# Gate and up blocks of the second feed-forward as Strassen units of seven half-size products

## Time and profile before

| | us |
|---|---|
| median of 3 runs | 1340.04 |
| lowest, highest | 1339.39, 1341.31 |
| span of the profiled execution | 1339.4 |
| its own time | not stated on the page; the median is 0.6 above the span |
| TensorE busy | 1322.1 (99%) |
| VectorE, ScalarE, GpSimd busy | 639.0, 418.3, 279.9 |

### The profile page before, as it was taken

One profiled execution on the slowest core, in us unless ns is written; L12 is line 12 of the kernel. 1 busy time (PEld: TensorE's weight loads), 2 busy tenths in 40 slices (PEclk: granted clock), 3 DMA queues, 4 the chain that ended last, 5 costly groups with the idle time before them and its releaser, 6 DMA issues.

```text
span 1339.4 us, 24243 instructions
## 1 busy us (share of the span) xinstructions
PE 1322.1 (99%) x10659; PEld 1285.2 (96%) x10659; DVE 639.0 (48%) x790; ACT 418.3 (31%) x577; POOL 279.9 (21%) x388
## 2 busy tenths in 40 slices
PE   7999999999999999999999999999999999999997
PEld 6999999999999999999999986899999999999997
DVE  4445246543644636468574546344433334433343
ACT  6222122221223422474434133333221122212233
POOL 0000789988702201000013000130000000000011
PEclk9999999999999999999999999999999999999998
DMA  6533332222223342126334747122322232222221
GB/s 185 111 83 96 86 88 79 80 82 84 88 64 95 84 83 61 48 80 163 103 93 130 242 179 247 37 80 81 91 81 79 80 90 84 79 79 83 79 60 71
DMA packets 227144, 130.24 MB, mean 97 GB/s; under 512 B 22240, under 2 KB 221392, under 8 KB 227024
## 3 DMA queue, kind: packets, MB, share of 16 engines
q1 hardware_dynamic: 223168, 123.66, 32.2%
q10 hardware_dynamic: 3872, 5.04, 1.1%
HBM read 121.72 MB, written 5.78 MB: 95 GB/s over the span
## 4 chain that ended last, share of the span: by engine, by line
PE 95%; DVE 2%; ACT 1%; issue 1%; DMA 0%; SPq 0%; DVEq 0%; ACTq 0%
PE PS L642 92%; PE PS L1183 1%; DMA AR<-in_x_prompt 0%; PE PS L719 0%; ACT wh L1315 0%; ACT gua L1375 0%; DVE Hs L1903 0%; PE PS L1161 0%; PE PS L801 0%; PE PS L1134 0%; DVE AR L2203 0%; PE PS L1269 0%; PE PS L812 0%; PE PS L866 0%; DVE Hs L1828 0%
## 5 line engine op out<-in xcount | busy, mean ns | idle before, releaser
L1315 ACT ACTIVATE wh<-raw 128x1024 fp32r<-128x1024 f32 (+1 forms) x192 | 200.3, 1043 | 742.0 <-PE PS L642 742.0
L642 PE MATMUL PS<-xh,wh 128*128 128x288 f32 x1792 | 390.9, 300 | 0.1
L642 PE MATMUL PS<-xh,wl 128*128 128x288 f32 x1792 | 384.2, 296 | 0.0
L642 PE MATMUL PS<-xl,wh 128*128 128x288 f32 x1792 | 384.0, 296 | 0.0
L642 PEld LDWEIGHTS PS<-xh,wh 128*128 128x128 f32 x1792 | 288.4, 189 | 2.6 <-issue 1.1
L642 PEld LDWEIGHTS PS<-xh,wl 128*128 128x128 f32 x1792 | 289.2, 189 | 0.0
L642 PEld LDWEIGHTS PS<-xl,wh 128*128 128x128 f32 x1792 | 289.0, 189 | 0.0
L1681 DVE TENSOR_TENSOR wl<-raw,wh 128x1024 fp32r<-128x1024 f32 (+1 forms) x192 | 245.9, 1280 | 73.9 <-ACT wh L1315 72.8
L642 PE MATMUL PS<-yh,wh 128*128 128x288 f32 x960 | 206.5, 297 | 0.0
L642 PE MATMUL PS<-yh,wl 128*128 128x288 f32 x960 | 205.6, 296 | 0.0
L642 PE MATMUL PS<-yl,wh 128*128 128x288 f32 x960 | 205.4, 296 | 0.0
(11 more groups left out here) (315 smaller groups left out, 988.0 us busy)
## 6 DMA issues: line engine op xcount, KB each, us to landing
raw<-in_w_ffn_gu SPq DMA_DIRECT2D x88, 512.0 KB, 3.8
raw<-in_w_ffn_down SPq DMA_DIRECT2D x32, 512.0 KB, 4.0
raw<-in_w_in SPq DMA_DIRECT2D x16, 512.0 KB, 4.0
raw<-in_w_ckv SPq DMA_DIRECT2D x16, 512.0 KB, 3.8
raw<-in_w_ffn_down SPq DMA_DIRECT2D x16, 384.0 KB, 3.4
Hs<-in_cache_mem_k SPq DMA_DIRECT2D x6, 1024.0 KB, 6.2
raw<-in_w_out SPq DMA_DIRECT2D x8, 512.0 KB, 4.1
raw<-in_w_cq SPq DMA_DIRECT2D x8, 512.0 KB, 4.5
```

Of the source, the lines that this page charges most:

```text
L642: return e.matmul(out, lhsT, rhs, start=start, stop=stop, **kw)
L1315: e.activation(wh[:, n % 2, 0:K * P], raw[:, n % 4, 0:K * P], ACT.Copy).then_inc(w_hi, 1)
```

## The change

Each pair of a gate and an up block of FFN2 becomes a **unit**. Its matrix is seen as two by two: low and high half of k (four tiles each) against gate and up; the tokens as low and high half of k against low and high half of the tokens (288). Seven products of half k and half the tokens (`product`, 4 x 3 matmuls of 288 columns) replace eight.

- Weight combinations: GpSimd forms four sums of 128 x 512 per unit (`weight_sums`), two units ahead; ScalarE rounds seven operands of 512 into a ring of ten (`weight_high`) and VectorE subtracts (`weight_low`), one unit ahead.
- Token combinations: four per k tile (`tok_h`, `tok_l`), formed once by VectorE during `w_co` (`norm3`), split by `tokens_high` and `tokens_low`.
- Results: products accumulate in banks 0 to 3; ScalarE copies intermediate states of bank 0 three times and of bank 1 once (`keep`: e1, e5, e2, e3), VectorE adds (`unit`). `gs` is multiplied by R as before, `us` is not: GpSimd multiplies `act` by R instead (`gate_by_root`).
- `xh` and `xl` of the low half of k hold only the low half of the tokens; `rms(3)` moves behind the fourth product of unit 0, and on ScalarE behind all splits of unit 1.
- `load` waits for the unit's splits and sums. Block counters skip the units (`seq`). 23 semaphores that were used once are merged into three counters, one per engine (`POINT`), counted in the order of their engine; the waits stand where they stood.

In the diff the indentation is cut by eight columns.

```diff
+RING, HK = 10, KD // 2
+ring_h = [view(ARr, 16 * T + 1024 * i, HK, P) for i in range(RING)]
+ring_l = [view(ARr, 16 * T + 1024 * i + 512, HK, P) for i in range(RING)]
+ring_hf = [t.bitcast(F32) for t in ring_h]
+xg = view(MM, 7168, HK, T)
+tok_h, tok_l = view(ARr, 0, HK, 4, TH), view(ARr, 8 * T, HK, 4, TH)
+tok_hf, tok_f = tok_h.bitcast(F32), view(AR, 8 * T, HK, 4, TH)
+spare = [view(Xs, i * KD * T, KD, T)[:, 0:HK, TH:T] for i in range(2)]
+sum1, sum2, sum3, sum4 = (spare[i // 2][:, :, i % 2 * P:i % 2 * P + P] for i in range(4))
+e1, e2, e3, e5 = (sq[:, i // 2, i % 2 * TH:i % 2 * TH + TH] for i in range(4))
...
-        add("gu", A[f"w_ffn{which}_gu"], 2 * nf, KD, 0, (f0 * P, F + f0 * P, P), f0=f0 + (which - 1) * FT)
+        add("gu", A[f"w_ffn{which}_gu"], 2 * nf, KD, 0, (f0 * P, F + f0 * P, P), f0=f0 + (which - 1) * FT, seven=which == 2)
...
+def seq(n):
+    return sum(1 for g, i in blocks[0:n] if not g.get("seven"))
+units = [n for n, (g, i) in enumerate(blocks) if g.get("seven") and i % 2 == 0]
+FIRST_UNIT = [0]
+for nf in FGROUPS:
+    FIRST_UNIT.append(FIRST_UNIT[-1] + nf)
...
-        if n >= 4:
-            e.wait_ge(w_lo, n - 1)
+        if n >= 4 and (n - 4) // 2 * 2 in units:
+            v = units.index((n - 4) // 2 * 2)
+            e.wait_ge(S("lo_ok"), 7 * v + (7 if n % 2 else 3))
+            e.wait_ge(S("sum_ok"), 4 * v + 4)
+        elif n >= 4:
+            e.wait_ge(w_lo, seq(n - 4) + 3)
...
+    def weight_sums(v, gate_times_r=None):
+        g, u = units[v], units[v] + 1
+        g_lo, g_hi = (raw[:, g % 4, a:a + 512].rearrange("p (k n) -> p k n", k=HK) for a in (0, 512))
+        u_lo, u_hi = (raw[:, u % 4, a:a + 512].rearrange("p (k n) -> p k n", k=HK) for a in (0, 512))
+        e.wait_ge(raw_in[g % 4], 16 * (g // 4 + 1))
+        e.wait_ge(raw_in[u % 4], 16 * (u // 4 + 1))
+        if v:
+            e.wait_ge(S("lo_ok"), 7 * v - 5)
+        TTT(sum1, u_lo, u_hi, ALU.add).then_inc(S("sum_ok"), 1)
+        e.wait_ge(S("sum_ok"), 4 * v + 1)
+        if v:
+            e.wait_ge(S("lo_ok"), 7 * v - 3)
+        TTT(sum2, sum1, g_lo, ALU.subtract).then_inc(S("sum_ok"), 1)
+        e.wait_ge(S("sum_ok"), 4 * v + 2)
+        if v:
+            e.wait_ge(S("lo_ok"), 7 * v - 2)
+        TTT(sum4, g_hi, sum2, ALU.subtract).then_inc(S("sum_ok"), 1)
+        if gate_times_r is not None:
+            gate_by_root(gate_times_r)
+        if v:
+            e.wait_ge(S("lo_ok"), 7 * v - 1)
+        TTT(sum3, g_lo, u_lo, ALU.subtract).then_inc(S("sum_ok"), 1)
+    def gate_by_root(v):
+        e.wait_ge(g_act, FT + v + 1)
+        TTT(act[:], act[:], R[:], ALU.mult).then_inc(S("act_r"), 1)
+    sums(3, between=lambda: weight_sums(0))
+    for i in range(3):
+        if i:
+            weight_sums(FIRST_UNIT[i])
+        weight_sums(FIRST_UNIT[i] + 1)
+        for v in range(FIRST_UNIT[i], FIRST_UNIT[i + 1]):
+            if v + 2 < FIRST_UNIT[i + 1]:
+                weight_sums(v + 2, gate_times_r=v)
+            else:
+                gate_by_root(v)
     sums(4)
...
+    def product(m, b, x_h, x_l, begins, ready=None):
+        e.wait_ge(S("lo_ok"), m + 1)
+        for k in range(HK):
+            if ready:
+                e.wait_ge(ready[0], ready[1] + k + 1)
+            for wi, (w, x) in enumerate(((ring_h, x_h), (ring_h, x_l), (ring_l, x_h))):
+                last = mm(bank(b, TH), w[m % RING][:, k, :], x[:, k, :], start=begins and k == 0 and wi == 0,
+                          stop=k == HK - 1 and wi == 2, skip_group_check=True)
+        last.then_inc(S("pr_done"), 1)
+    def unit(v):
+        n, first = units[v], v in FIRST_UNIT
+        lo, hi, lo_t, hi_t = slice(0, HK), slice(HK, KD), slice(0, TH), slice(TH, T)
+        if first:
+            e.wait_ge(ps_free, seq(n) + 1)
+        e.wait_ge(S("e_ok"), 4 * v)
+        product(7 * v, 0, xh[:, lo, lo_t], xl[:, lo, lo_t], True, ready=(x_lo, 24) if v == 0 else None)
+        if v:
+            e.wait_ge(S("c_ok"), 4 * v - 2)
+        product(7 * v + 1, 1, tok_h[:, :, 0, :], tok_l[:, :, 0, :], True, ready=(S("t1_lo"), 0) if v == 0 else None)
+        if first:
+            e.wait_ge(ps_free, seq(n) + 2)
+        if v:
+            e.wait_ge(S("c_ok"), 4 * v - 3)
+        product(7 * v + 2, 3, xh[:, hi, lo_t], xl[:, hi, lo_t], True, ready=(x_lo, 28) if v == 0 else None)
+        e.wait_ge(S("e_ok"), 4 * v + 1)
+        product(7 * v + 3, 0, tok_h[:, :, 2, :], tok_l[:, :, 2, :], False, ready=(S("t_lo"), 0) if v == 0 else None)
+        if v == 0:
+            rms(3)
+        e.wait_ge(S("e_ok"), 4 * v + 2)
+        product(7 * v + 4, 1, xh[:, hi, hi_t], xl[:, hi, hi_t], False)
+        e.wait_ge(S("e_ok"), 4 * v + 3)
+        product(7 * v + 5, 0, tok_h[:, :, 1, :], tok_l[:, :, 1, :], False)
+        if v:
+            e.wait_ge(S("c_ok"), 4 * v)
+        product(7 * v + 6, 2, tok_h[:, :, 3, :], tok_l[:, :, 3, :], True)
+    for i, nf in enumerate(FGROUPS):
+        for v in range(FIRST_UNIT[i], FIRST_UNIT[i + 1]):
+            unit(v)
+        g, v = groups[FFN2 + 2 * i + 1], FIRST_UNIT[i + 1]
+        for b in range(KD):
+            if b == 0:
+                e.wait_ge(S("e_ok"), 4 * v)
+                e.wait_ge(S("c_ok"), 4 * v - 2)
+            elif b == 1:
+                e.wait_ge(S("c_ok"), 4 * v)
+            dense(g["n0"] + b, b % 2, nf, yh, yl, ready=(hid_lo, FT + FIRST_UNIT[i]) if b == 0 else None,
+                  each=turn_last if i == 2 and b == KD - 1 else None)
...
+    def weight_high(v, j):
+        g, u, m = units[v], units[v] + 1, 7 * v + j
+        src = (raw[:, g % 4, 0:512], sum1, raw[:, g % 4, 512:1024], sum2, sum4, sum3, raw[:, u % 4, 512:1024])[j]
+        if j in (0, 2):
+            e.wait_ge(raw_in[g % 4], 16 * (g // 4 + 1))
+        elif j == 6:
+            e.wait_ge(raw_in[u % 4], 16 * (u // 4 + 1))
+        else:
+            e.wait_ge(S("sum_ok"), 4 * v + (0, 1, 0, 2, 3, 4)[j])
+        if m >= RING:
+            e.wait_ge(S("pr_done"), m - RING + 1)
+        if j in (0, 2, 6):
+            src = src.rearrange("p (k n) -> p k n", k=HK)
+        e.activation(ring_h[m % RING], src, ACT.Copy).then_inc(S("hi_ok"), 1)
+    def next_high(v, j):
+        if v + 1 < len(units) and v + 1 not in FIRST_UNIT:
+            weight_high(v + 1, j)
+        elif j in (1, 4):
+            conv(units[v] + 2 + j // 3)
+    def tokens_high(k):
+        kk = k % HK
+        if k < HK:
+            e.wait_ge(S("t_sum"), kk + 1)
+            e.activation(tok_h[:, kk, 0, :], tok_f[:, kk, 0, :], ACT.Copy).then_inc(S("t_hi"), 1)
+        else:
+            e.wait_ge(S("t_sum"), HK + 3 * kk + 3)
+            e.activation(tok_h[:, kk, 1:4, :], tok_f[:, kk, 1:4, :], ACT.Copy).then_inc(S("t_hi"), 1)
+    def norm3(k):
+        e.wait_ge(ps_free, groups[W_O]["n0"] + k + 3)
+        if 16 + k > 1:
+            e.wait_ge(acc_ready, 16 + k - 1)
+        e.activation(sq[:, k % 2, :], chunk(h, k), ACT.Square).then_inc(sq_ready, 1)
+        gain = gains[:, G_FFN2, k:k + 1]
+        if k < HK:
+            e.activation(xg[:, k, :], h[:, k, :], ACT.Copy, scale=gain).then_inc(S("xg_ok"), 1)
+            e.activation(xh[:, k, 0:TH], h[:, k, 0:TH], ACT.Copy, scale=gain).then_inc(x_hi, 1)
+        else:
+            e.activation(xh[:, k, :], h[:, k, :], ACT.Copy, scale=gain).then_inc(x_hi, 1)
     e.wait_ge(kv_out, 64)
-    group(W_O, norm3)
-    ffn(FFN2, 3)
+    n0 = groups[W_O]["n0"]
+    for k in range(KD):
+        if k < KD - 2:
+            conv(n0 + k + 2)
+        if k >= HK:
+            weight_high(0, 2 * k - 8)
+            if k < KD - 1:
+                weight_high(0, 2 * k - 7)
+        if k:
+            tokens_high(k - 1)
+        norm3(k)
+    tokens_high(KD - 1)
+    def keep(v, i, done, out, b):
+        e.wait_ge(S("pr_done"), 7 * v + done)
+        if v:
+            e.wait_ge(S("c_ok"), 4 * v - 4 + i)
+        e.activation(out, bank(b, TH), ACT.Copy).then_inc(S("e_ok"), 1)
+    def unit(v):
+        if v == 0:
+            e.wait_ge(S("t_lo"), HK)
+            e.wait_ge(acc_ready, 24)
+        keep(v, 1, 1, e1, 0)
+        next_high(v, 0)
+        if v and v not in FIRST_UNIT:
+            hidden_high(v - 1)
+        keep(v, 3, 2, e5, 1)
+        for j in (1, 2):
+            next_high(v, j)
+        keep(v, 2, 4, e2, 0)
+        for j in (3, 4):
+            next_high(v, j)
+        if v == 0:
+            for j in (5, 6):
+                next_high(v, j)
+            rms(3)
+        keep(v, 4, 6, e3, 0)
+        if v:
+            next_high(v, 5)
+        e.wait_ge(g_scaled, FT + v + 1)
+        if v:
+            e.wait_ge(hid, FT + v)
+        e.activation(act[:], gs[:], ACT.Silu).then_inc(g_act, 1)
+        if v:
+            next_high(v, 6)
+    def hidden_high(v):
+        e.wait_ge(hid, FT + v + 1)
+        f = v - max(x for x in FIRST_UNIT if x <= v)
+        e.activation(yh[:, f, :], us[:], ACT.Copy).then_inc(hid_hi, 1)
+    for i in range(3):
+        for v in range(FIRST_UNIT[i], FIRST_UNIT[i + 1]):
+            unit(v)
```

(103 more changed lines are left out.)

167 lines of the change are left out of this document (92 added, 75 removed).

## The result

The changed kernel takes 1349.32 us (median of 4 runs, 1349.28 to 1350.61) beside 1340.67 (1339.39 to 1341.52) for the one before: a ratio of 1.0066, 95% interval 1.0052 to 1.0080. It is slower by about 9 us where 6 us less were forecast.

The account below looks back on a forecast made before the run. TensorE's number of matmuls was taken as the bound. Removed matmuls -35.2, stalls +18.8, entry +8.0 and +2.3 sum to -6.1 us: 1334 us against the median 1340.04, range 1308 to 1348.

Parts of the forecast that it names:

- Removed, -35.2: TensorE in the FFN2 units: 264 fewer matmuls at 0.133 us each, with no loss of pace, -35.2 us.
- rival 3: TensorE's products break the matmul stream, 0.08 us at each of 154 product starts: 1346 us, chance 0.07.
- rival 4: The change does not do what it says, still 96 matmuls a unit: 1340 us, chance 0.02.
- What the mechanism is: In the units, GpSimd's SBUF reads block VectorE; TensorE's fifth product then waits for ScalarE's bank 1 copy once lag passes 5.2 us.
- One unit of VectorE, 12.7: VectorE's round per FFN2 unit takes 12.7 us against TensorE's 11.2, so it falls behind 1.5 us per unit.
- The blocked part: Time per unit in which VectorE's operations with two SBUF inputs are held up by GpSimd's reads: 4.75 us.
- Its own part: VectorE's own operations in a unit, 7.8 us, with 0.15 us of waiting for ScalarE.
- Stalls, 18.8 + 16 (L - 12.7): TensorE's waits in the three groups of units, sixteen units with sums: +18.8 us at a VectorE loop of 12.7.
- L: Length of VectorE's loop per unit in us: taken as 12.7, bounds 11.2 (cover holds) and 14.1 (nothing overlaps).
- The entry, +10.3: From w_co's last blocks to unit 1: +8 us before the fourth product, +2.3 us before unit 1.
- lies between 9.9 and 11.1, the last token split ends at 12.2: VectorE's `xl` and last token split, in us from the end of w_co's last block; fourth product then starts at 12.7.
- rival 2: VectorE's and GpSimd's SBUF operations exclude each other from start to end: loop 14.05 us, 1358 us in all, chance 0.14.

Follow-up runs that it names:

- e1: The changed kernel with GpSimd's four sums of a unit replaced by memsets of the same 512 columns, sums left out of the computation: 1312.2 us (one run).
- e3: The changed kernel with ScalarE copying bank 1 out ahead of the previous unit's high half of the hidden block: 1346.3 us, ratio 1.0039.
- e4: The changed kernel with VectorE's sums of a unit in idle PSUM banks 4 to 7 instead of SBUF: 1327.0 us, ratio 0.9894.
- e6: e4 with the gate's multiplication by R moved from GpSimd to VectorE and SiLU applied in place in PSUM: 1320.2 us, ratio 0.9849.
- e5: The changed kernel with GpSimd's sums for the second unit begun only after VectorE made the last token halves: 1346.2 us, ratio 1.0047.
- e9: e7 with 40 throwaway matmuls on an idle bank in TensorE's gaps of unit 0: 1316.2 us, ratio 0.9817.
- e7: e6 with e3, e5 and, in unit 0, the third norm's root and a bank 0 copy ahead of the last two weight blocks: 1316.3 us, ratio 0.9821.
- e8: e7 with the last residual block's token halves and lows first on VectorE and ScalarE, the seventh weight block behind: 1317.0 us, ratio 0.9820.
- e11: e9 with ScalarE's roots of the third norm and a bank 0 copy ahead of unit 1's fourth and fifth weight blocks: 1318.3 us, ratio 0.9828.

## Why the prediction was wrong

**Removed, -35.2:** right. 264 matmuls, 0.133 us apart, no break at a product's start; rival 3 is out, and rival 4.

**What the mechanism is:** right, link by link (e1, e3 and e4 between them rule out the rivals that were named): a gap ahead of the fifth product, ended by the copy of bank 1, behind the high half, behind `us` x act; splits of 512 up to 1.91. e1 takes GpSimd's reads away and the gaps go, e4 and e6 take away part of what meets them and the round falls with it.

**One unit of VectorE, 12.7:** mis-sized, measured 13.21. The blocked part was near, 4.85 against 4.75. Its own part was 8.35 against 7.95. I let every operation begin 0.08 us before the last ends. The rows show where it doesn't: `gs` x R begins at 952.69, 0.04 behind the end of the half it reads, and `us` x act at 959.24, 0.03 behind; the split at 948.98 has no overlap either; and the wait for ScalarE is 0.22, not 0.15. These and the blocked part make 0.5 us, and it counts sixteen times: 8.2 us by the prediction's own formula.

**Stalls, 18.8 + 16 (L - 12.7):** at the measured L the formula gives 27.0, the trace 31.0. 3.0 of the rest is a term I didn't have. After some stalls the clock falls, once in each group. Windows of TensorE around the last stall of the first:

```profile
984.00:988.00 4.00, 2.32 (x18) 2.09 (x16) 3.75 (x5) 0.92 (x3) 2.43 (x2) 1.00 0.36 106
988.00:992.00 4.00, 3.88 (x18) 3.89 (x19) 4.00 (x6) 2.44 (x6) 1.28 (x1) 0.58 0.10 29
```

From 988 on eighteen matmuls fill 3.88 us, where the windows at 2.4 GHz hold 32. In the second group the timeline has 36 matmuls from 1152.24 to 1158.66, 6.42 us in place of 4.79: 1.6 us. It is lost where no stall follows, in the second and the third group (units 14 and 20 take 14.72 us, their neighbours 13.21). In the first group it cost nothing: the next stall was shorter by the same amount, and the two units together take 26.4, twice 13.2:

```profile
1001.31 0.40 PE L716 MATMUL PS<-xh,ARr 128*128 128x288 f32 x1 [0.26 <-ACT sq L1827]
```

TensorE would have waited there for VectorE's round in any case. The last 1.0 us of the 31.0 is not assigned.

**The entry, +10.3:** measured +14.2 (the forecast's times, too, hold the mean squares in unit 0: unit 1 at 22.4, measured 26.4). The step that failed here is "lies between 9.9 and 11.1, the last token split ends at 12.2". It ended at 15.8, and the fourth product came 16.3 us behind the start of unit 0, not 12.7. I counted GpSimd's first four sums and the `acc` addition, and forgot that the second unit's sums follow at once and fall beside the last block's chain of short dependent operations. e5 takes them away there, and the fourth product comes at 12.7, the forecast's own number. From the fourth product to unit 1 the forecast was 9.7, the trace shows 10.2; the half clock over this stretch is not what cost, as e9 shows for e7's order (for the changed kernel's own order it wasn't tried).

**The sum and the range.** With 27.0 for the stalls, 3.0 for the clock and 14.2 for the entry the same sum is +9.0; w_co's +0.6, the unassigned 1.0 and the end's -1.1 make it +9.5, and the spans differ by 9.4. The forecast was -6.1, and 1349.3 lies just above the range's upper end, 1348. From -6.1 to +9.0 the sum missed 15.1 us: 8.2 by a round that was taken 0.5 us too short, 3.9 at the entry, 3.0 by the clock. The first alone would have given +2, the second alone -2, both +6. The prediction gave the point itself: from L = 13.1 the gain is gone (with its own entry), and it put 13.1 at the edge of its range. An excess over TensorE's 11.2 of 1.5 us was known to a third at best, and a term multiplied by 16 deserved ends of 12.0 and 14.1, and a larger chance for rival 2. (The forecast's own range was also added up loosely: 13.1 and an entry of 10 give 1342, not 1344.) That rival named the right side and the right mechanism, but its own price (1358, no overlap at all) did not come: 0.12 to 0.15 us do overlap at each change.

## What to carry to other kernels

Before work is moved to VectorE and GpSimd "beside" TensorE, add up one round of the pair as if each two-input VectorE operation from SBUF and each reading GpSimd operation excluded the other (less the 0.12 to 0.15 us of overlap measured here at each change), with waits between dependent operations included, and compare it with TensorE's round; where it comes out near, a few tenths of a microsecond a round decide the sign. What relieves it is cheap: put VectorE's intermediate results in idle PSUM banks, so that each of its operations has one SBUF input, and take short multiplications off GpSimd even at the price of more VectorE work; here these two turned +9 us into -20 (e6), and with the repairs of the entry into -24 (e7). At the place where such a phase begins, list what every engine still has in its queue: in e8 to e11 each repair of the entry moved the wait to the next link and gained nothing.

## What was not expected of the hardware

- TensorE's granted clock fell to 1.2 GHz for some 3.4 us in the middle of a busy phase: behind gaps of 1.78 us that came every 13.2 us, not at the first but at a late one of each group (the fifth at 988.12 and 1152.24, the third at 1278.24). e5 has gaps of 1.78 to 1.84 and other places: the third and the fifth of the first group (959.26, 985.67), the fourth of the second (1136.65), none of the third. In e3, with gaps of up to 1.75 us every 13.1 us, and in e4, with some 0.54, the clock stays at 1.00 in units 1 to 21. So the place can't be told ahead from these runs, and the cost is nothing where another stall follows.
- A VectorE operation with two SBUF inputs that begins during a GpSimd read ends at that read's end plus its lone time less 0.12 to 0.15 us. In the changed kernel from 940 to 1300 us that holds for all 82 such operations of the units. A GpSimd read that begins inside such a VectorE operation is held in the same way (60 of 60, less 0.07 to 0.16). It holds whether the GpSimd instruction has two inputs (a split of 1.73 beside 1.30) or one (0.96 beside 0.83).
- GpSimd's `act` x R of 576 takes 1.43 us alone where 1.24 was taken from the multiplications in the earlier trace rows; its memset of 512 takes 0.53.
